# Forgetting attention scored in two fp32r products of split q and k, head by head

## The reference, cut to what matters

```
def forgetting_attention(q, k, v, log_f):
    F = jnp.cumsum(log_f, axis=1).transpose(0, 2, 1)
    ...
    def block(args):
        qi, Fi, s0 = args                     # qi is scaled by Dh ** -0.5
        s = jnp.einsum('bhqd,bhkd->bhqk', qi, kh)
        s = s + Fi[..., None] - F[:, :, None, :]
        qpos = s0 + jnp.arange(Q_BLOCK, dtype=jnp.int32)
        s = jnp.where(key_pos[None, :] <= qpos[:, None], s, NEG)
        p = jax.nn.softmax(s, axis=-1)
        return jnp.einsum('bhqk,bhkd->bhqd', p, vh)
```

## Time and profile before

| what | value |
|---|---|
| median of 3 runs | 1985.2 us |
| lowest, highest | 1983.4, 1986.08 us |
| the profiled execution: its time | 1987.4 us |
| its span in the profile | 1986.1 us |
| busy in the span: PE, PEld | 98%, 80% |
| busy: DVE, ACT, POOL | 54%, 45%, 44% |
| granted TensorE clock, mean | 0.995 |
| fp32 score products (line 1410) | 96 records, 1387.9 to 1584.8 us |

### The profile page before, as it was taken

How to read it: one execution, slowest core, us unless ns; L and a number is a source line. 1 busy time by engine, 2 the same in 40 slices (tenths; PEclk the granted TensorE clock), 3 DMA queues, 4 the chain that set the end, 5 groups by cost and what they waited for, 6 DMA issues and landing times.

```text
span 1986.1 us, 28017 instructions
## 1 busy us (share of the span) xinstructions
PE 1938.2 (98%) x11035; PEld 1587.4 (80%) x11035; DVE 1079.4 (54%) x1802; ACT 898.9 (45%) x1713; POOL 877.3 (44%) x672
## 2 busy tenths in 40 slices
PE   5999999999999999999999999999999999999998
PEld 4868787878788877888888888888688778888886
DVE  5577879695466645664544440345765576511114
ACT  3555656564455544233444342344655454422223
POOL 1323333233533326564454444454474461655543
PEclk9999999999999999999999999999999999999999
DMA  8255353533322117664333324336123323433231
GB/s 307 65 171 183 108 190 117 182 125 120 96 69 60 44 40 292 226 227 159 96 97 94 105 83 150 98 115 186 52 76 84 78 59 106 159 98 95 89 110 70
DMA packets 92322, 242.41 MB, mean 122 GB/s; under 512 B 28192, under 2 KB 31392, under 8 KB 90784
## 3 DMA queue, kind: packets, MB, share of 16 engines
q1 hardware_dynamic: 88784, 231.98, 37.1%
q10 hardware_dynamic: 3408, 8.65, 1.1%
HBM read 223.14 MB, written 14.29 MB: 120 GB/s over the span
## 4 chain that ended last, share of the span: by engine, by line
PE 92%; DVE 2%; ACT 2%; SPq 1%; DMA 1%; POOL 1%; issue 1%; ACTq 0%; DVEq 0%
PE ps L943 23%; PE ps L944 23%; PE ps L952 22%; PE ps L1273 3%; PE ps L1348 2%; PE ps L1335 2%; PE ps L1323 1%; PE ps L1250 1%; PE ps L1410 1%; PE ps L1007 1%; PE ps L1014 1%; PE ps L1008 1%; DMA modwb<-in_w_mod 1%; PE ps L947 1%; PE ps L1429 1%; PE ps L1233 1%
## 5 line engine op out<-in xcount | busy, mean ns | idle before, releaser
L2843 POOL TENSOR_TENSOR wlo<-raww,whi 128x512 fp32r<-128x512 f32 x207 | 282.3, 1364 | 688.7 <-ACT whi L1475 688.2
L1475 ACT CAST whi<-raww 128x1024 fp32r<-128x1024 f32 (+2 forms) x279 | 279.4, 1006 | 174.3 <-PE ps L952 146.6
L2844 POOL TENSOR_TENSOR wlo<-raww,whi 128x512 fp32r<-128x512 f32 x207 | 284.2, 1373 | 0.0
L943 PE MATMUL ps<-hT_h,whi 128*128 128x512 f32 (+1 forms) x688 | 252.7, 377 | 1.2 <-ACT whi L1475 0.6
L944 PE MATMUL ps<-hT_l,whi 128*128 128x512 f32 (+1 forms) x688 | 245.6, 366 | 0.0
L943 PE MATMUL ps<-H_h,whi 128*128 128x512 f32 x480 | 189.4, 395 | 0.6 <-DVE sq L2075 0.4
L944 PE MATMUL ps<-H_l,whi 128*128 128x512 f32 x480 | 187.1, 390 | 0.0
L952 PE MATMUL ps<-hT_h,wlo 128*128 128x512 f32 (+1 forms) x688 | 152.0, 363 | 0.0
L943 PEld LDWEIGHTS ps<-hT_h,whi 128*128 128x128 f32 x688 | 130.4, 190 | 25.9 <-issue 3.4
L944 PEld LDWEIGHTS ps<-hT_l,whi 128*128 128x128 f32 x688 | 130.5, 190 | 22.3 <-issue 1.9
L2075 DVE SCALAR_TENSOR_TENSOR gt<-gt,ps 128x512 f32<-128x512 f32 x40 | 27.5, 688 | 200.6 <-PE ps L952 177.6
(11 more groups left out here) (590 smaller groups left out, 4417.5 us busy)
## 6 DMA issues: line engine op xcount, KB each, us to landing
ec<-csd SPq DMA_DIRECT2D x32, 1024.0 KB, 8.1
raww<-in_w_up SPq DMA_DIRECT2D x44, 512.0 KB, 3.5
modr<-in_w_mod SPq DMA_DIRECT2D x32, 512.0 KB, 5.7
raww<-in_w_xbc SPq DMA_DIRECT2D x24, 512.0 KB, 3.9
raww<-in_w_gl SPq DMA_DIRECT2D x24, 512.0 KB, 3.6
raww<-in_w_z SPq DMA_DIRECT2D x16, 512.0 KB, 3.7
raww<-in_w_g SPq DMA_DIRECT2D x16, 512.0 KB, 3.6
raww<-in_w_os SPq DMA_DIRECT2D x16, 512.0 KB, 3.9
```

What stands on the lines that cost most here:

```text
L943: e.matmul(o, whi[:, i, c], hi(k)[:, t0:t1], start=(k == 0), stop=False)
L1475: e.copy(o, x.rearrange("p (k c) -> p k c", c=64) if p == plan.first["dt", 0] else x).then_inc(*w_high.mark(("high", p)))
L2843: e.tensor_tensor(o[:, 0:512], x[:, 0:512], h[:, 0:512].bitcast(F32), ALU.subtract).then_inc(*p_wlow.mark(("first half", p)))
L2844: e.tensor_tensor(o[:, 512:1024], x[:, 512:1024], h[:, 512:1024].bitcast(F32), ALU.subtract).then_inc(*p_wlow.mark(("split", p), ("raw fre ...
```

## The change

- Each head gets one GEMM whose 128 output features are its 64 q and its 64 k features (`w_fqk` is reordered on the host). There are 12 such GEMMs as before.
- Scores become two fp32r matmuls: the first multiplies the stack (q high; q low) by (k high; k high), the second (ones and zeros; q high) by (forget rows and zeros; k low). The mask's matmul stays. The product of the two low parts is left out. Four operands per head (`Q_STACK`, `Q_HIGH`, `K_TWICE`, `K_LOW`) in buffers for two heads replace two operands in buffers for four.
- `("fqout", h)` now is on ACT two conversions from PSUM, and on DVE two subtractions from PSUM that wait for ACT's two. The bank is free after both. `("fqdup", h)` is two ACT copies within SBUF. SP issues two DMAs per head for the forget sum's high and low part; `("frows",)` makes these parts once.
- `head_by_head` rewrites the list: `fqout h+1` stands right after `fscore h, 1` and `fqdup h+1` right after `fscore h, 2`, for h from 1 to 10. `u 5` moves to where `fq 1` was. `fq 11` comes where `qm 0` was, followed by `gf 3`, and `qm 0`, `qm 1` and `qm 2` come one head later each or more.

With this list the GEMM `fq h+1` precedes the scores of head h, and the steps that take its bank again are, for h+1 from 2 to 11: `fscore 1,3`; `fscore 2,3`; `fscore 3,3`; `tm w_fv 1,0`; `fpt 4,1`; `fpt 5,3`; `fscore 7,2`; `fpt 7,2`; `fpt 8,2`; `fscore 10,2`. The order around head 7 is: `fq 8`, `fpv 2`, `s5k 1`, `s5u 3`, `s5x 1`, `fout 2`, `gf 2`, `s5rot 1`, `gfout 2`, `fscore 7,0`, `fpt 6,1`, `fscore 7,1`, `fqout 8`, `fpt 6,0`, `fscore 7,2`, `fqdup 8`, `s5scan 1`, `fpt 6,2`, `fscore 7,3`.

```diff
-    return o
+    return head_by_head(o)
+
+
+def head_by_head(o):
+
+    heads = {0: 0, 6: 1, 7: 2, 2: 3, 8: 4, 3: 5, 9: 6, 4: 7, 10: 8, 5: 9, 11: 10}
+    out = []
+    for s in o:
+        if s in (("u", 5), ("fqout", 1), ("gf", 3), ("gfout", 3), ("qm", 1), ("qmout", 0), ("qmout", 1), ("qmout", 2)):
+            continue
+        if s == ("fq", 1):
+            out.append(("u", 5))
+        elif s[0] in ("fq", "fqout"):
+            h = heads[s[1]]
+            if s[0] == "fq":
+                out.append(("fq", h))
+            elif h < 2:
+                out += [("fqout", h), ("fqdup", h)]
+        elif s == ("tmout", "w_fv", 0, 2):
+            out += [s, ("frows",)]
+        elif s[0] == "fscore" and s[2] in (1, 2) and 1 <= s[1] <= 10:
+            out += [s, ("fqout" if s[2] == 1 else "fqdup", s[1] + 1)]
+        else:
+            out += {("qm", 0): [("fq", 11), ("gf", 3), ("gfout", 3)], ("qm", 2): [("qm", 0), ("qmout", 0), ("qm", 1), ("qmout", 1)],
+                    ("qm", 3): [("qm", 2), ("qmout", 2), s]}.get(s, [s])
+    return out
 
...
-        qk = sbuf("qk", [P, 2, 4, L], 114)
+        qk = sbuf("qk", [P, 2, 4, L], 114, F32R)
...
-        FT = sbuf("FT", [12, L], 162)
+        FT = sbuf("FT", [44, L], 162, F32R)
...
-        fqk = lambda h, i: qk[:, h // 2 % 2, 2 * i + h % 2, :]
+        fqk = lambda h, i: qk[:, h % 2, i, :]
+        Q_STACK, Q_HIGH, K_TWICE, K_LOW = 0, 1, 2, 3
...
-                        PE.wait_ge(at("fq", h // 2))
-                        PE.wait_ge(at("fq", 6 + h // 2))
+                        PE.wait_ge(at("fq twice", h))
+                        PE.wait_ge(at("fq low", h))
                         PE.wait_ge(at("forget row", h))
                         PE.wait_ge(at("rows of ones"))
 
                     for i, a in {0: ((0, 0), (1, 128)), 1: (), 2: ((2, 0),), 3: ((3, 0),)}[n]:
                         Wd = (i + 1) * 128
-                        e.matmul(ps[:, b, a:a + Wd], fqk(h, 0)[:, i * 128:(i + 1) * 128], fqk(h, 1)[:, 0:Wd], start=True, stop=False)
+                        e.matmul(ps[:, b, a:a + Wd], fqk(h, Q_STACK)[:, i * 128:(i + 1) * 128], fqk(h, K_TWICE)[:, 0:Wd], start=True, stop=False)
+                        e.matmul(ps[:, b, a:a + Wd], fqk(h, Q_HIGH)[:, i * 128:(i + 1) * 128], fqk(h, K_LOW)[:, 0:Wd], start=False, stop=False)
                         e.matmul(ps[:, b, a + i * 128:a + Wd], maskb[:, 0, :], maskb[:, 2, :], start=False, stop=True).then_inc(
...
                 elif k == "fqout":
-                    m, src = s[1], ("fq", s[1])
-                    i, b = m // 6, bank_of((src, 0))
+                    h, src = s[1], ("fq", s[1])
+                    b = bank_of((src, 0))
                     ACTE.wait_ge(at("gemm", src, 0))
-                    if m % 6 >= 2:
-                        for h in (2 * (m % 6) - 4, 2 * (m % 6) - 3):
-                            ACTE.wait_ge(at("fscores", h, 3))
-                    for h in (0, 1):
-                        e.mul(fqk(2 * (m % 6) + h, i)[0:64, :], ps[64 * h:64 * h + 64, b, :], 1.0 if i else 0.125).then_inc(
-                            *a_moved.mark(*[("out of", (src, 0)), ("fq", m)] * h))
+                    if h >= 2:
+                        ACTE.wait_ge(at("fscores", h - 2, 3))
+                    e.mul(fqk(h, Q_STACK)[0:64, :], ps[0:64, b, :], 0.125).then_inc(*x_high.mark(("fq high", h)))
+                    e.copy(fqk(h, K_TWICE)[64:128, :], ps[64:128, b, :]).then_inc(*x_high.mark(("fk high", h), ("out of", (src, 0))))
+                elif k == "fqdup":
+                    h = s[1]
+                    ACTE.wait_ge(at("fk high", h))
+                    e.copy(fqk(h, Q_HIGH)[64:128, :], fqk(h, Q_STACK)[0:64, :].bitcast(F32)).then_inc(*x_high.mark())
+                    e.copy(fqk(h, K_TWICE)[0:64, :], fqk(h, K_TWICE)[64:128, :].bitcast(F32)).then_inc(*x_high.mark(("fq twice", h)))
+                elif k == "frows":
+                    ACTE.wait_ge(at("forget sums"))
+                    e.copy(FT[0:12, :], ffs[:, 2, :]).then_inc(*x_high.mark(("forget high",)))
...
-                    e.tensor_tensor_scan(FT[:, :], ones[0:12, 0:1].to_broadcast([12, L]), fl, 0.0, ALU.mult, ALU.add).then_inc(
+                    e.tensor_tensor_scan(fn, ones[0:12, 0:1].to_broadcast([12, L]), fl, 0.0, ALU.mult, ALU.add).then_inc(
                         *v_made.mark(("forget sums",)))
+                elif k == "frows":
+                    DVE.wait_ge(at("forget high"))
+                    e.tensor_tensor(FT[32:44, :], ffs[:, 2, :], FT[0:12, :].bitcast(F32), ALU.subtract).then_inc(*v_made.mark(("forget rows",)))
+                elif k == "fqout":
+                    h, src = s[1], ("fq", s[1])
+                    b = bank_of((src, 0))
+                    DVE.wait_ge(at("fq high", h))
+                    e.scalar_tensor_tensor(out=fqk(h, Q_STACK)[64:128, :], in0=ps[0:64, b, :], scalar=0.125, in1=fqk(h, Q_STACK)[0:64, :].bitcast(F32),
+                                           op0=ALU.mult, op1=ALU.subtract).then_inc(*v_xlow.mark())
+                    DVE.wait_ge(at("fk high", h))
+                    e.tensor_tensor(fqk(h, K_LOW)[64:128, :], ps[64:128, b, :], fqk(h, K_TWICE)[64:128, :].bitcast(F32), ALU.subtract).then_inc(
+                        *v_xlow.mark(("fq low", h), ("out of", (src, 0))))
...
-                    e.memset(qk[64:128, :, :, :].rearrange("p a b c -> p (a b c)"), 0.0).then_inc(*p_step.mark())
-                    after_last()
-                    for i in (0, 1):
-                        e.memset(qk[64:65, i, 0:2, :].rearrange("p b c -> p (b c)"), 1.0).then_inc(*p_made.mark(*[("rows of ones",)] * i))
+                    for h in (0, 1):
+                        e.memset(fqk(h, Q_HIGH)[0:64, :].bitcast(F32), 0.0).then_inc(*p_step.mark())
+                        e.memset(fqk(h, K_LOW)[0:64, :].bitcast(F32), 0.0).then_inc(*p_step.mark())
+                    after_last()
+                    for h in (0, 1):
+                        e.memset(fqk(h, Q_HIGH)[0:2, :].bitcast(F32), 1.0).then_inc(*p_made.mark(*[("rows of ones",)] * h))
...
-                elif k in ("forget", "fqout"):
-
-                    m = s[1] if k == "fqout" else 0
-                    if k == "forget":
-                        SP.wait_ge(at("forget sums"))
+                elif k == "frows" or k == "fqout" and s[1] >= 2:
+
+                    if k == "frows":
+                        SP.wait_ge(at("forget rows"))
                         SP.wait_ge(at("rows of ones"))
-                    if k == "forget" or 0 < m < 6:
-                        for h in (2 * m, 2 * m + 1):
-                            if h >= 4:
-                                SP.wait_ge(at("fscores", h - 4, 3))
-                            e.dma_start(fqk(h, 1)[64:65, :], FT[h:h + 1, :]).then_inc(*f_row[h % 4].mark(("forget row", h)))
+                    for h in (0, 1) if k == "frows" else (s[1],):
+                        if h >= 2:
+                            SP.wait_ge(at("fscores", h - 2, 3))
+                        for i in (0, 1):
+                            e.dma_start(fqk(h, K_LOW)[i:i + 1, :].bitcast(F32), FT[32 * i + h:32 * i + h + 1, :].bitcast(F32)).then_inc(
+                                *f_row[h % 4].mark(*[("forget row", h)] * i))
...
-    arr["w_fqk"] = blocks(w[:, 0:1536])
+    arr["w_fqk"] = blocks(_np.concatenate([w[:, 0:768].reshape(1024, 12, 64), w[:, 768:1536].reshape(1024, 12, 64)], axis=2).reshape(1024, 1536))
```

## The result

The change makes the kernel slower: 2045.7 us, median of four runs (2043.4 to 2047.25), against 1985.6 of four runs of the kernel before, a ratio of 1.030 (95% interval 1.028 to 1.032). The profiled execution took 2047.25 us with a span of 2045.5, 59.4 above the span before. The forecast was 2019 us in a range of 1995 to 2041: the right side, but 27 us too low and outside the range.

What follows compares the result with a forecast made beforehand. TensorE was taken to bound the kernel; -9.6 (scores) + 41.9 (bank waits) - 3.3 (old idle times gone) + 5 (clock) = +34 us on the profiled 1987.4, so 2021.4, median 2.2 below: 2019 us, range 1995 to 2041.

Steps and rivals of the forecast that it cites:

- the term for the clock: TensorE's clock drops after stalls: of ten, the four longest may each cost 1.7 us; +5, between 0 and +17.
- The saving: Scores on TensorE: 0.80 us saved per head, times 12, -9.6 us; bounds -7 and -12.
- The cost of the added operations: Conversions 0.59 us, SBUF copies 0.55, subtractions 0.69 each; 13 us of copies and 17 of subtractions fit in spare time.
- The case that POOL slows them: VectorE's subtractions beside POOL: each would cost 1.1 us more, 2.2 a head, as in a 1.81 us row.
- The wait and its size: TensorE waits for the bank of the next head's GEMM, free 3.80 us after the maxima begin; ten heads, +41.9 us.
- What I put at nothing: Row DMAs, POOL's clearing, forget rows made once, and `u 5` in `fq 1`'s place: no cost.
- rival 3: Every stall drops TensorE's clock (+12 us more), or subtractions meet POOL (+2.2 x 10): 2031 to 2041 us; chance 0.12.
- old ones gone: TensorE's two idle times of the kernel before, ahead of head 4's scores and the value GEMM, vanish: -3.3 us.
- the one in which the bank comes in time: Rival: VectorE and ScalarE free the bank early enough, only the saving is left: 1975.6 us; chance 0.10.
- half the stalls: Rival: delays give VectorE and ScalarE a lead that carries to the next head, 21 us of stalls: 1995 us; chance 0.20.
- the change does what it says: Denies a rival: fp32r score products run at the fp32 rate, +4 us for 128 columns, +37 for all; chance 0.03.
- More than the sum: The same as rival 3; its first branch is that every stall drops TensorE's clock, +12 us more; chance 0.12.

Runs made afterwards that it cites:

- early_out: The change, but conversions, subtractions and SBUF copies of each next head stand ahead of the current head's scores, where the kernel before had its copies; 2007.0 us.
- first_out_sooner: early_out, but the conversions and subtractions of heads 0 and 1 stand ahead of the S5 preparation in VectorE's queue; 2002.5 us.
- change_first_out: The change, with only the conversions and subtractions of heads 0 and 1 moved ahead of the S5 preparation; 2039.9 us.
- late_3_and_10: early_out, but for heads 4 and 11 the conversions and subtractions stand behind the second score step, as in the change; 2015.2 us.

## Why the prediction was right or wrong

The mechanism and the places of the waits came as predicted, the time did not. Of the 25 us by which the stretch grew beyond the forecast 34, 17 are the term for the clock, 6.6 two waits that were priced at nothing and 4.4 the sizes of the ten waits; 2.7 went the other way.

**The saving: right, somewhat smaller than forecast.** TensorE's timeline of head 0's scores:

```profile
1390.44 0.22 PE L1436 MATMUL ps<-qk 128*128 128x128 f32 x1
1390.50 0.28 PE L1437 MATMUL ps<-qk 128*128 128x128 f32 x1
...
1391.50 0.48 PE L1436 MATMUL ps<-qk 128*128 128x512 f32 x1
1391.82 0.40 PE L1437 MATMUL ps<-qk 128*128 128x512 f32 x1
1392.05 0.23 PE L1438 MATMUL ps<-maskb 128*128 128x128 bf16 x1
1392.10 0.48 PE L969 MATMUL ps<-H_h,whi 128*128 128x512 f32 x1
```

1392.10 - 1390.44 = 1.66 us against 2.52: 0.86 saved where I had 0.80. But head 0 is the best case. The score and mask matmuls of all twelve heads, from start to start without idle times and at full clock, take 30.3 us before, 21.4 in the change and 22.2 in early_out: 8.1 to 8.9 us saved against 9.6. The 512-column product took 0.32 and 0.23 us from start to start (I had 0.24 each), the 128-column one 0.06 and 0.12, a mask 0.05.

**The cost of the added operations: right.** Groups by line in the stage (out<-in, count, busy and mean ns, idle before):

```profile
L1832 ACT CAST qk<-qk 64x512 fp32r<-64x512 f32 x10 | 6.2, 617 | 0.2
...
L1827 ACT CAST qk<-ps 64x512 fp32r<-64x512 f32 x10 | 5.8, 581 | 0.2
...
L2741 DVE TENSOR_TENSOR qk<-ps,qk 64x512 fp32r<-64x512 f32 x10 | 6.9, 694 | 0.3
L2738 DVE SCALAR_TENSOR_TENSOR qk<-ps,qk 64x512 fp32r<-64x512 f32 x10 | 6.8, 684 | 12.4 <-ACT qk L1826 12.4
```

0.62 us for a copy (taken 0.55), 0.58 for a conversion (0.59), 0.69 for a subtraction (0.69), though POOL was busy 9.5 of the 10 us around head 3's (1443 to 1453). The case that POOL slows them, at 1.81 us each, did not come: with one PSUM input they run as line 2075 does. Line 2773, with two SBUF inputs, first beside a busy POOL, then beside an idle one:

```profile
1438.60 1.78 DVE L2773 TENSOR_TENSOR yf<-sq,yf 128x512 f32<-128x512 f32 x1
...
1533.89 0.69 DVE L2773 TENSOR_TENSOR yf<-sq,yf 128x512 f32<-128x512 f32 x1
```

The subtraction took 0.69 us at 1447.94, beside a busy POOL. The Trainium skill ("SBUF — State Buffer", section "SBUF: two separate sides") says that a VectorE instruction takes the pair of ports that it shares with GpSimd only in a two-port fast mode or with two SBUF inputs beside a GpSimd instruction that reads SBUF; the trace agrees by these three times.

**The wait and its size: right.** VectorE's maxima of head 7 and its last subtraction, and between them ScalarE's normalisation:

```profile
1534.50 0.62 DVE L2093 TENSOR_REDUCE smf<-ps 128x1 f32<-128x128 f32 x2
...
1537.64 0.69 DVE L2741 TENSOR_TENSOR qk<-ps,qk 64x512 fp32r<-64x512 f32 x1
...
1536.02 0.39 ACT L1541 ACTIVATE Pf<-Pf,smf 128x128 f32<-128x128 f32 x1
```

From 1534.50 to 1537.64 + 0.69 it is 3.83 us; the prediction had 3.80. By head, forecast and measured:

| head | 1 | 2 | 3 | 4 | 5 | 6 | 7 | 8 | 9 | 10 | sum |
|---|---|---|---|---|---|---|---|---|---|---|---|
| forecast | 2.6 | 2.6 | 9.5 | 2.4 | 4.9 | 2.4 | 4.7 | 2.4 | 2.4 | 8.0 | 41.9 |
| measured | 3.47 | 3.27 | 12.11 | 2.07 | 4.83 | 2.07 | 4.73 | 2.32 | 2.70 | 8.77 | 46.3 |

4.4 us short, 2.6 of it at head 3.

**What I put at nothing: wrong for one step.** The prediction put `u 5` in `fq 1`'s place at nothing since the next GEMM covers it, and did not ask where VectorE comes to head 0's subtractions. They stand behind the S5 preparation, and the value GEMM waits for them: 5.45 us and a dip of 2.4. first_out_sooner and change_first_out show this part. The move also took a GEMM away from in front of the value GEMM; one GEMM takes 5.4 us (`fq 0` and `fq 1` start at 1354.82 and 1360.26), so with `u 5` in its old place the wait would have been about covered. This part is worked out from those two starts; no run shows it. Another 1.10 us at 1399.76 comes from head 0's transpose, early against its normalisation. The row DMAs cost nothing, as predicted: no idle time is ended by them.

**The clock: wrong, and the largest error (17 of the 25 us).** The step was: "Of ten stalls, the four longest may each cost 1.7 us and some not: +5". Windows behind two of the waits, columns as above, the clock third from the end:

```profile
1403.00:1411.00 8.00, 6.25 (x17) 4.69 (x18) 6.09 (x24) 5.14 (x13) 0.00 (x0) 0.57 0.16 56
1609.00:1615.00 6.00, 5.96 (x27) 5.68 (x28) 1.21 (x3) 2.30 (x5) 0.00 (x0) 0.50 0.00 0
```

0.50 of full speed is 1.2 GHz. There are ten dips in the change, behind the 5.45 us wait and behind nine of the ten bank waits (all but head 4's 2.07); each cost 1.5 to 3.0 us, 22.1 in all, where I had 5. I had argued from the two gaps of 1.93 and 1.34 us in the stage before, behind which the clock stayed at 1.00, that most stalls would go free. The value in the earlier trace rows (1.7 us a dip) was near the 2.2 measured, the number of dips was not: most of the error is that six more waits had one. The top of the range did not hold it either, since rival 3 added only 12 us for the clock and nothing for longer or unseen waits. The rule that I set beside it is that idle waits between bursts throttle the engine again (the Trainium skill, "TensorE: Matmul & The Clock Gate", section "HAM oscillation — how this bites in real kernels"). The trace agrees for ten of the twelve waits of 1 us and more, the shorter ones of 2.07 to 2.70 us among them; the clock stayed at 1.00 behind the 1.10 us and behind head 4's 2.07.

In sum, by the stretch: waits 46.3 (41.9), the two unseen ones 6.6 (0), old ones gone -3.6 (-3.3), clock 22.1 (5), saved -12 (-9.6): 59 for 34. What is saved beyond the scores' 8.9 us is not assigned to a line.

Of the rivals, the one in which the bank comes in time was refuted by the ten waits; half the stalls likewise, and by late_3_and_10, where single waits had their full size; the change does what it says. "More than the sum" is what happened, by its first branch, but beyond that rival's 2041 us too: its clock of 17 us in all fell short of the 22.1, and it had neither the two unseen waits nor the longer ones.

## What to carry to other kernels

When a copy is moved behind other work in an engine's queue, look for who takes its source's buffer next: here a place one or two steps later cost 39 us, though VectorE was busy for 55% of the stage and ScalarE for 47%. Price waits of TensorE of such lengths (2 to 12 us) with a dip of its clock on top (here 2.2 us each), and look at the queue order of the engine that frees the buffer before counting its spare time. A wait that is removed often gives way to one behind it, so gains of single mends do not add.

## What was not expected of the hardware

- The same idle time did not always have the same price: 1.93 us ahead of head 4 left the clock at 1.00 in the kernel before, and so did 2.07 us at 1462.73 in the change; but 2.07 us at 1515.28 was followed by over 3 us at half speed, and in change_first_out so was head 4's wait, 2.08 us there. What TensorE did around them differs; the runs do not tell which part of that decides.
- In early_out, waits of 0.62 and 1.26 us within 1.6 us (at 1488.99 and 1490.56) were followed by a dip, the clock's mean over 1490 to 1497 being 0.76. In late_3_and_10 the same pair (0.61 and 1.27 us) was not. The number of dips of a kernel is thus no simple count of its waits, and with some 2 us each it moves the time by as much as the smaller mends here.
- Kernels with the same instructions up to there reached the forget branch at 1350.5 to 1354.8 us. The cause is open; differences of under 4 us between medians of different kernels should not be read without the trace.
